# Two transformer blocks: the sums of squares shared between GpSimd and TensorE

## Chip, cores and metric

One core of one Trainium2 chip. The metric is the device time of one execution in microseconds.

## What is computed

Two transformer blocks of two layers each run one after the other on 512 tokens of width 1024 (the first also carries 256 context tokens in its first layer). Everything is fp32, and each large product is made of three matmuls on parts of the operands ("high" and "low"). Around every mixer and every feed-forward layer stand norms over the 1024 features of a token:

```
def rms_norm(x, g):
    xf = x.astype(jnp.float32)
    y = xf * lax.rsqrt(jnp.mean(xf * xf, axis=-1, keepdims=True) + EPS)
    return (y * g.astype(jnp.float32)).astype(x.dtype)

def modulate(x, g, shift, scale):
    return rms_norm(x, g) * (1 + scale) + shift
...
    h = h + gt_m * rms_norm(y, g_post_m)
    f = conv_ffn(modulate(h, g_pre_f, sh_f, sc_f), w_up[layer], ...)
    h = h + gt_f * rms_norm(f, g_post_f)
```

The second block's sliding-window attention adds a bias by distance, `rel_table[t5_bucket(rel)]`, which this kernel builds as a sum of 31 steps, each a `Sign` of the distance.

## The kernel before

**Layout.** Features lie on the partitions, in eight tiles of 128 features each (`K.h`, `K.y`: 128 x 8 x tokens), tokens along the free dimension: `TX` = 512, or `T0` = 768 with the context. A token's sum of squares therefore runs over eight tiles and over the partitions.

**Phases.** The program is a list of `Phase` objects. Each engine runs its own part of every phase in the order of that list, and counts of semaphores tie the parts together. Every engine is thus an in-order queue: what TensorE has in the next phase stands behind what it has in this one.

**Weights.** A chunk of 128 x 1024 weights is loaded by SyncE into one of six raw buffers (`load_chunk`), rounded by ScalarE to the high part (`split_hi`, L214) and subtracted by GpSimd to the low part (`split_lo`, L222). There are three buffers each for the high and the low parts (`HL`), so that chunk c+3 can be split once chunk c was used. TensorE waits for the low part (`chunk_ops`). L236 to L238 are the three matmuls of a large product. In the last layer before a norm some of these splits are put off behind the norm's root (`split_after`).

**Squares of the norms that this change touches.** `InnerNorm` (a norm of the layer's output, then the residual add, then the next norm) and `PreNorm` (the next norm alone) both inherit from `Squares`. There are nine. ScalarE squares tile k into a ring of two (768 tokens) or three (512) buffers in `K.t1` (`squared`, L674). GpSimd adds the eight squares one by one into `K.rstd` (`add`: L683 the first two, L686 each further one), and counts them in `y_used` or `sq_used`, on which ScalarE waits before it overwrites a buffer. Then TensorE makes one true fp32 product of `K.rstd` with a matrix of 1/1024 (`summed`, L700), which sums over the partitions and gives every partition the mean; and ScalarE takes the first root from PSUM (`first_root`, L709). VectorE improves it (L774, L780, L782 in `InnerNorm`, L846, L848, L850 in `PreNorm`) and makes the x tiles (L450, L459), each of which frees one step of the next layer's first product.

The squares are made while the layer before still ends. In a `Proj` phase (the output projections, and others) ScalarE's loop reads product i out of PSUM (L2645, where there is no gate), squares tile i and splits chunk i+3; with a gate VectorE reads the product (L867), and ScalarE splits first and squares tile i-1. GpSimd's loop adds square i-1 and then splits chunk i+3. After a feed-forward layer (`Ffn`) all eight squares follow VectorE's reads of the last eight products (L1309 or L867) inside `first_root` and `pool`.

The nine: after the even mixer's projection (768 tokens, root at 463 us), after its feed-forward layer (768, 1075), after the attention's projection (512, 1480), after that feed-forward layer (512, 1872), and five `PreNorm`: after a feed-forward layer at 2264, 2999 and 3374, after the projection with a gate at 2623 and 3729.

In `InnerNorm` TensorE goes on with `hold` (L165) and then the second norm's squares, one product each (L756). `warm` (L157) are matmuls whose result nobody reads: 22 of them at 512 tokens, in three groups, the second behind the first root and the third behind VectorE's first product; they stand ahead of the first product of the next layer.

**Signs.** `BiasTable(K, heads, tables, during, plan)`: ScalarE makes the 31 signs (L2082) in groups between its reads of the products of phase `during`; `plan[0]` before the first, `plan[i+1]` after product i. VectorE folds each into the sum (L2124). For the first table that phase is the projection of the values, with four products (L2650 reads them). For its third product TensorE needs a chunk that ScalarE splits after the second product, behind the signs of the first.

Of the kernel before, what the change touches and what calls it, by code (L numbers as in the profile page):

```python
# [29 lines left out]
TX = 512  # L30
TC = 256
T0 = TX + TC
# [30 lines left out]
def parts(T):  # L63

    return [(0, TX)] if T == TX else [(0, TX), (TX, TC)]
# [1 line left out]

EXTRA_SEMS = ["pe_gained", "mla_r", "qn_ready", "qc_ready", "gn_ready", "ang_ready", "cs_ready", "bias_ready", "bias_kept", "z_ready",
              "st_abs", "st_e", "st_nl", "a_ready", "lg_ready", "st_exp", "so_ready", "st_done", "mw_in", "rpb_in",
              "st_used", "table_in", "y_sq", "y_used", "y_total", "sq_total", "sq_sq", "mix_sq", "mix_total", "mix_r0", "mix_read", "mix_done", "begun_hi", "begun_lo", "rel_ready", "sign_ready", "sign_used"]  # L70
AREA = 4 * 4 * T0 + 3072


class Phase:
# [3 lines left out]
    def __init__(self, K):  # L78
        self.K, self.sem = K, K.sem
        self.base, self.c_next = dict(K.total), len(K.chunks)  # L80
        counts = self.counts()
        self.ring_before, K.ring_now = K.ring_now, None
        if "out_ready" in counts:
            K.ring_now = self.ring_T
        for name, n in counts.items():
            K.total[name] = K.total.get(name, 0) + n
        K.phases.append(self)

    def counts(self):
        return {}  # L90

    def at(self, name, n=0):

        return self.base.get(name, 0) + n
# [79 lines left out]
    def act(self, e): pass  # L174
    def dve(self, e): pass
    def pool(self, e): pass
# [30 lines left out]
def split_hi(K, act, c, n=0):  # L207
    if c >= len(K.chunks):
        return
    _, a, b, _ = K.chunks[c]  # L210
    act.wait_ge(K.sem[f"raw_in{c % RAW}"], 16 * (c // RAW + 1) + n * (16 * LC // RAW))
    if c >= HL:
        act.wait_ge(K.sem["out_ready"], K.chunks[c - HL][3] + n * LT)
    act.activation(K.whi[:, c % HL, 0:a * b], K.raw[:, c % RAW, 0:a * b], ACT.Copy).then_inc(K.sem["w_hi"], 1)  # L214


def split_lo(K, pool, c, n=0):
    if c >= len(K.chunks):
        return
    _, a, b, _ = K.chunks[c]  # L220
    pool.wait_ge(K.sem["w_hi"], c + 1 + n * LC)
    pool.tensor_tensor(K.wlo[:, c % HL, 0:a * b], K.raw[:, c % RAW, 0:a * b],  # L222
                       K.whi[:, c % HL, 0:a * b].bitcast(F32), ALU.subtract).then_inc(K.sem["w_lo"], 1)
# [188 lines left out]
class Modulated(Phase):  # L412
# [3 lines left out]
    def product(self, k):  # L416
        n = 2 if self.T == T0 else 3
        a = k % n * self.T
        return self.K.t2[:, :, :].rearrange("p a t -> p (a t)")[:, a:a + self.T]
# [45 lines left out]
class Norm(Modulated):  # L465
# [25 lines left out]
    def rstd_free(self, act):  # L491
        pass
# [156 lines left out]
class Squares:  # L649
# [2 lines left out]

    def begin(self, kind):
        self.kind, self.added, self.done, self.split_after = kind, 0, 0, []

    def square(self, k):
        n, T = (2, self.T) if self.T == T0 else (3, self.T)
# [2 lines left out]
    def squared(self, e, k):  # L662
        K, n = self.K, 2 if self.T == T0 else 3
        if k < 0:
            return
        if k == 0:
            e.preload_act_table_set("abs_reciprocal_sqrt_and_small")
            e.wait_ge(self.sem["act_lo"], self.act_lo)
        self.done = k + 1
        self.tile_done(e, k)  # L670
        if k >= n:
            used = self.kind + "_used"
            e.wait_ge(self.sem[used], self.at(used, k - n + 1))
        e.activation(self.square(k), self.tile(k), ACT.Square).then_inc(self.sem[self.kind + "_sq"], 1)  # L674

    def add(self, e, k):
        if k < 0:
            return
        self.added = k + 1
        acc, used = self.K.rstd[:, 0:self.T], self.kind + "_used"  # L680
        e.wait_ge(self.sem[self.kind + "_sq"], self.at(self.kind + "_sq", k + 1))
        if k == 1:
            e.tensor_tensor(acc, self.square(0), self.square(1), ALU.add).then_inc(self.sem[used], 2)  # L683
        elif k > 1:
            e.wait_ge(self.sem[used], self.at(used, k))
            e.tensor_tensor(acc, acc, self.square(k), ALU.add).then_inc(self.sem[used], 1)  # L686

    def pool(self, e):
        for k in range(self.added, 8):
            self.add(e, k)  # L690
        for c in self.split_after:
            split_lo(self.K, e, c)

    def summed(self, e):

        e.wait_ge(self.sem["ada_read"], self.ada_read)
        e.wait_ge(self.sem["bias_ready"], self.at("bias_ready"))
        e.wait_ge(self.sem[self.kind + "_used"], self.at(self.kind + "_used", 8))
        for a, w in parts(self.T):
            ins = e.matmul(self.total()[:, a:a + w], self.K.mean_d[:, :], self.K.rstd[:, a:a + w], start=True, stop=True)  # L700
        ins.then_inc(self.sem[self.kind + "_total"], 1)

    def first_root(self, e):

# [9 lines left out]
class InnerNorm(Squares, Norm):  # L714
# [2 lines left out]


    def __init__(self, K, T, post, pre, out):
        super().__init__(K, T, post, pre)  # L720
        self.act_lo, self.ada_read, self.tile_done, out.norm = self.at("act_lo"), K.ada_tasks, self.y_read, self
        self.begin("y")

    def counts(self):
        c = super().counts()
        c.update(self.ring_counts(self.T, 1))
        c.update(sq_ready=8, sq_used=7, y_sq=8, y_used=8, y_total=1)
        return c

    def total(self):  # L730
# [76 lines left out]
class PreNorm(Squares, Modulated):  # L807
# [2 lines left out]


    def __init__(self, K, pre):
        self.T, self.pre = TX, [pre]
        super().__init__(K)
        self.tile_done, self.ada_read, self.act_lo = K.h_done, K.ada_tasks, self.at("act_lo")
        self.begin("sq")
        K.phases[-2].norm = self

    def counts(self):
        return dict(sq_sq=8, sq_used=8, sq_total=1, r0_ready=1, xm_full=8, xm_hi=8, x_ready=8)  # L820

    def total(self):
        return self.K.pf[:, 6 * BANK:7 * BANK]
# [47 lines left out]
class Proj(Phase):  # L871
# [146 lines left out]
    def act(self, e):  # L1018
        T = self.T
        if self.table:  # L1020
            self.table.after(e, -1)
        for i, ((_, n, _, read), tok, own) in enumerate(self.products):
            if tok is None:
                if self.gate:
                    self.next_weights(e, i)
                    self.norm.squared(e, i - 1)
                    continue
                e.wait_ge(self.sem["out_ready"], self.at("out_ready", i + 1))
                read(e, self.slot(T, i)).then_inc(self.free(T, i), 1)
                if self.norm:  # L1030
                    self.norm.squared(e, i)
                self.next_weights(e, i)
                if self.table:
                    self.table.after(e, i)
            else:
                e.wait_ge(self.sem["out_ready"], self.at("out_ready", i + 1))
                for c in own if tok else ():
                    split_hi(self.K, e, c + HL)
                src = self.slot(T, i).rearrange("p (t c) -> p t c", t=self.half)[:, :, 0:n]
                read(e, src, tok).then_inc(self.free(T, i), 1)  # L1040
                if self.table:
                    self.table.after(e, i)
# [1387 lines left out]
class MlaNorm(Phase):  # L2430
# [40 lines left out]
    def pe(self, e):  # L2471
# [35 lines left out]
        while done < 9:  # L2507
            add(done)
            done += 1
# [138 lines left out]
def tokens_to(dst, col, func=ACT.Copy):  # L2648

    return lambda e, src, t: e.activation(dst[:, t:t + src.shape[1], col:col + src.shape[2]], src, func)  # L2650
# [11 lines left out]
def build(nc, io, out, stop=None):  # L2662
    K = Keep()
# [4 lines left out]
    with ExitStack() as ctx:  # L2668
# [54 lines left out]
        n = 4 * T0  # L2723
# [23 lines left out]
        def proj(T, w, jobs, wait=None, cls=Proj, **kw):  # L2747
            ph = cls(K, T, w, jobs, **kw)
            ph.warmed = wait is x_ready
            if wait:  # L2750
                ph.x_wait = lambda e, k: wait(ph, e, k)
            return ph
# [15 lines left out]
        first_table, first_pos = [at(4 * n, TX)], at(4 * n + 2560, TX).bitcast(I32)  # L2768
# [10 lines left out]
        proj(T0, w_in, jobs, tasks=mods[EARLY:5])  # L2779
        GmlpMix(K, gated)  # L2780
        v = proj(T0, w_in, [(2048 + g * 256, 256, True, tokens_to(K.vtok, g * 256)) for g in range(2)])
        table = BiasTable(K, [0], first_table, v, (0, 12, 12, 7))
        table.pos, table.posf = first_pos, at(4 * n + 2048, TX)
        split = Split(K, [K.sT[:, g, :] for g in range(4)], T0, "ya_done")

# [236 lines left out]
def finish(K, nc, out):  # L3022

    Store(K, out, out.shape[1])
    with nc.Block() as block:
        @block.sync
        def _(sp):
            for ph in K.phases:
                ph.sp(sp)

        @block.tensor
        def _(pe):
            for ph in K.phases:
                ph.pe(pe)

        @block.scalar
        def _(act):
            for ph in K.phases:
                ph.act(act)

        @block.vector
        def _(dve):
            for ph in K.phases:
                ph.dve(dve)

        @block.gpsimd
        def _(pool):
            for ph in K.phases:
                ph.pool(pool)
# [120 lines left out]
```

## Time and profile before

| what | us |
|---|---|
| runs before (3) | 4100.53, 4103.48, 4104.28; median 4103.48 |
| the profiled execution | 4102.06 |
| its span, first to last instruction | 4100.3 |
| TensorE busy, matmul | 3837.4 (94%) |
| VectorE, ScalarE, GpSimd busy | 1888.1, 1480.9, 1615.6 |

The span is what the trace covers; 1.8 us of the execution's time lie outside it. Matmuls are pipelined, so a busy TensorE isn't one at its peak. "L700" is line 700 of the kernel.

### The profile page before, as it was taken

Reading aid. Unit: us, or ns where it says so; the run is one execution under the profiler, and the core shown is the slowest. Engines: PE = TensorE matmul, PEld = TensorE weight load, DVE = VectorE, ACT = ScalarE, POOL = GpSimd, SP = SyncE. Lnnn points to the kernel's source line nnn. Section 1 sums busy time; section 2 is a strip of 40 time slices with the busy share of each in tenths; the row PEclk is TensorE's granted clock in tenths of the full one; section 3 lists DMA queues with packets and bytes.
Section 4 is the critical chain, followed back from the end, with each engine's and each line's share of the span. In section 5 each row is a group of like instructions: output and inputs, shape, how many; then the busy total and the mean of one; then the engine's idle time right before and its main releaser. Section 6 shows DMA issues by size and latency. Waiting matters only on the chain. (4 is left out here: it accounts for less than half of the span.)

```text
span 4100.3 us, 52392 instructions
## 1 busy us (share of the span) xinstructions
PE 3837.4 (94%) x19218; PEld 3035.1 (74%) x19218; DVE 1888.1 (46%) x3264; ACT 1480.9 (36%) x2293; POOL 1615.6 (39%) x801
## 2 busy tenths in 40 slices
PE   6987899999898899999999899999999999899999
PEld 5866688888666668887888753788878877547887
DVE  3775866543645556655554845222232232452222
ACT  3264522222325663333222554322232233533222
POOL 1320253444330046654455321455555553115554
PEclk9999999999999999999999998999999999989999
DMA  7610144442110027763665310233323332102332
GB/s 248 193 37 24 52 129 128 145 131 61 36 47 19 1 76 230 227 198 113 225 217 167 84 47 1 67 98 93 96 83 97 97 90 66 42 1 82 97 98 77
DMA packets 460503, 411.96 MB, mean 100 GB/s; under 512 B 28096, under 2 KB 405312, under 8 KB 460352
## 3 DMA queue, kind: packets, MB, share of 16 engines
q1 hardware_dynamic: 457903, 408.65, 32.3%
q8 instruction: 92, 1.51, 0.2%
q10 hardware_dynamic: 2448, 1.32, 0.1%
q14 instruction: 60, 0.48, 0.0%
HBM read 406.25 MB, written 7.60 MB: 101 GB/s over the span
## 5 line engine op out<-in xcount | busy, mean ns | idle before, releaser
L222 POOL TENSOR_TENSOR s_wlo<-s_raw,s_whi 128x1024 fp32r<-128x1024 f32 x490 | 1181.6, 2419 | 1927.4 <-ACT s_whi L214 1925.9
L236 PE MATMUL psum<-s_xhi,s_whi 128*128 128x512 f32 x3264 | 1227.5, 376 | 20.6 <-POOL s_wlo L222 11.0
L237 PE MATMUL psum<-s_xlo,s_whi 128*128 128x512 f32 x3264 | 1219.9, 374 | 0.0
L238 PE MATMUL psum<-s_xhi,s_wlo 128*128 128x512 f32 x3264 | 1216.5, 373 | 0.0
L214 ACT ACTIVATE s_whi<-s_raw 128x1024 fp32r<-128x1024 f32 x490 | 510.1, 1056 | 1533.8 <-PE psum L238 1530.5
L236 PEld LDWEIGHTS psum<-s_xhi,s_whi 128*128 128x128 f32 x3264 | 615.6, 189 | 139.8 <-POOL s_wlo L222 13.4
L237 PEld LDWEIGHTS psum<-s_xlo,s_whi 128*128 128x128 f32 x3264 | 615.5, 189 | 111.4 <-issue 3.6
L238 PEld LDWEIGHTS psum<-s_xhi,s_wlo 128*128 128x128 f32 x3264 | 614.6, 188 | 111.9
L236 PE MATMUL psum<-s_ahi,s_whi 128*128 128x512 f32 x1232 | 469.0, 381 | 11.6 <-DVE s_y L1309 7.2
L238 PE MATMUL psum<-s_ahi,s_wlo 128*128 128x512 f32 x1232 | 464.8, 377 | 0.0
L237 PE MATMUL psum<-s_alo,s_whi 128*128 128x512 f32 x1232 | 462.4, 375 | 0.0
L1297 DVE TENSOR_TENSOR s_t<-psum,s_t 128x512 f32<-128x512 f32 x88 | 60.9, 692 | 842.0 <-ACT s_t L1255 842.0
L867 DVE SCALAR_TENSOR_TENSOR s_h<-psum,s_coef,s_h 128x512 f32<-128x512 f32 x368 | 268.8, 749 | 198.5 <-PE psum L238 184.6
L236 PEld LDWEIGHTS psum<-s_ahi,s_whi 128*128 128x128 f32 x1232 | 232.8, 189 | 58.1 <-DVE s_y L1309 7.8
L238 PEld LDWEIGHTS psum<-s_ahi,s_wlo 128*128 128x128 f32 x1232 | 232.7, 189 | 46.3
L237 PEld LDWEIGHTS psum<-s_alo,s_whi 128*128 128x128 f32 x1232 | 232.7, 189 | 44.4
L384 DVE CUSTOM_DVE_ANT_0 s_ada_raw<-s_ada_raw,psum 128x1024 f32<-128x1024 f32 x176 | 214.0, 1216 | 54.3 <-DMA s_ada_raw<-w_ada 43.8
L1285 DVE SCALAR_TENSOR_TENSOR s_t<-psum,s_cols,s_t 128x511 f32<-128x511 f32 (+1 forms) x132 | 82.9, 655 | 324.8 <-ACT s_t L1252 324.8
L1343 POOL TENSOR_TENSOR s_alo<-s_t,s_ahi 128x512 fp32r<-128x512 f32 (+1 forms) x132 | 183.5, 1390 | 37.4 <-ACT s_ahi L1262 37.4
L1623 PE MATMUL psum<-s_ident,s_t 128*128 128x128 f32 x772 | 131.7, 294 | 69.8 <-DVE s_t L1748 35.1
L1681 ACT ACTIVATE s_area<-psum 128x512 f32<-128x512 f32 (+1 forms) x212 | 123.1, 581 | 148.1 <-PE psum L1623 147.9
L1623 PEld LDWEIGHTS psum<-s_ident,s_t 128*128 128x128 f32 x772 | 84.8, 146 | 120.6 <-issue 65.1
(306 smaller groups left out, 4274.9 us busy)
## 6 DMA issues: line engine op xcount, KB each, us to landing
s_ada_raw<-w_ada SPq DMA_DIRECT2D x224, 512.0 KB, 3.9
s_raw<-w_gu SPq DMA_DIRECT2D x176, 512.0 KB, 3.8
s_raw<-w_up SPq DMA_DIRECT2D x88, 512.0 KB, 4.7
s_raw<-w_dn SPq DMA_DIRECT2D x88, 512.0 KB, 3.5
s_raw<-w_down SPq DMA_DIRECT2D x44, 512.0 KB, 4.6
s_raw<-w_in SPq DMA_DIRECT2D x30, 512.0 KB, 3.9
s_raw<-w_in_ab SPq DMA_DIRECT2D x20, 512.0 KB, 6.6
s_area<-w_first SPq DMA_DIRECT2D x16, 512.0 KB, 11.9
```

Of the source, the lines that this page charges most:

```text
L214: act.activation(K.whi[:, c % HL, 0:a * b], K.raw[:, c % RAW, 0:a * b], ACT.Copy).then_inc(K.sem["w_hi"], 1)
L222: pool.tensor_tensor(K.wlo[:, c % HL, 0:a * b], K.raw[:, c % RAW, 0:a * b], K.whi[:, c % HL, 0:a * b].bitcast(F32), ALU.subtract).then_inc ...
L236: pe.matmul(out, lh, rh, start=first, stop=False)
L237: pe.matmul(out, lh, rl, start=False, stop=False)
L238: return pe.matmul(out, ll, rh, start=False, stop=last)
L384: ins = dve.tensor_tensor_reduce(out=chunk if v == last else K.ada_acc[:, 0, :], in0=chunk, in1=self.rows.row(v), scale=1.0, scalar=0.0, o ...
L867: return e.scalar_tensor_tensor(out=K.h[:, m, 0:TX], in0=product, scalar=K.coef[:, m:m + 1], in1=K.h[:, m, 0:TX], op0=ALU.mult, op1=ALU.add)
L1285: ins = e.scalar_tensor_tensor(out=dst[:, a + 1:a + w], in0=src[:, a:a + w - 1], scalar=K.cols[:, bass.ds(c, 1)], in1=dst[:, a + 1:a + w], ...
L1297: e.tensor_tensor(K.t1[:, i, 0:T], self.slot(T, t - 1), K.t2[:, i, 0:T], ALU.mult).then_inc(self.sem["prod"], 1)
L1343: e.tensor_tensor(K.alo[:, j % 2, i, 0:T], K.t1[:, i, 0:T], K.ahi[:, j % 2, i, 0:T].bitcast(F32), ALU.subtract).then_inc(self.sem["act_lo" ...
L1623: ins = e.transpose(self.t(4)[:, i * P:(i + 1) * P], self.p(s, j)[:, b * P:(b + 1) * P], K.ident[:, :])
L1681: e.activation(self.pt(s, 4 * c, m), self.t(m), ACT.Copy).then_inc(self.sem["t_copied"], 1)
```

## The change

The first tiles' squares are still added by GpSimd: seven of them where the norm follows a projection (`Proj`), five after the feed-forward layer of 768 tokens, six after those of 512. TensorE multiplies the remaining squares with the matrix of 1/1024 itself and accumulates in PSUM. `order` says in which order TensorE takes them; `None` is GpSimd's sum. A new semaphore (`y_seen`, `sq_seen`) counts the squares that TensorE has read. In `Proj` without a gate ScalarE splits the next chunk before it squares the tile. The first table's signs are dealt out 0, 9, 14, 8 instead of 0, 12, 12, 7.

```diff
@@ class Squares
-    def begin(self, kind):
-        self.kind, self.added, self.done, self.split_after = kind, 0, 0, []
+    def begin(self, kind, adds):
+        self.kind, self.added, self.done, self.split_after, self.adds = kind, 0, 0, [], adds
+        self.order = {7: (None, 7), 6: (6, 7, None), 5: (5, 6, None, 7)}[adds]
+
+    def kind_counts(self):
+        return {self.kind + "_sq": 8, self.kind + "_used": self.adds, self.kind + "_total": 1,
+                self.kind + "_seen": sum(k is not None for k in self.order[:-1])}
@@ squared
         if k >= n:
-            used = self.kind + "_used"
-            e.wait_ge(self.sem[used], self.at(used, k - n + 1))
+            name, past = (self.kind + "_used", 0) if k - n < self.adds else (self.kind + "_seen", self.adds)
+            e.wait_ge(self.sem[name], self.at(name, k - n + 1 - past))
@@ add
-        if k < 0:
+        if k < 0 or k >= self.adds:
             return
@@ pool
-        for k in range(self.added, 8):
+        for k in range(self.added, self.adds):
@@ summed
-        e.wait_ge(self.sem[self.kind + "_used"], self.at(self.kind + "_used", 8))
-        for a, w in parts(self.T):
-            ins = e.matmul(self.total()[:, a:a + w], self.K.mean_d[:, :], self.K.rstd[:, a:a + w], start=True, stop=True)
-        ins.then_inc(self.sem[self.kind + "_total"], 1)
+        def product(x, first, last):
+            for a, w in parts(self.T):
+                ins = e.matmul(self.total()[:, a:a + w], self.K.mean_d[:, :], x[:, a:a + w], start=first, stop=last)
+            return ins
+
+        for k in self.order:
+            if k is None:
+                e.wait_ge(self.sem[self.kind + "_used"], self.at(self.kind + "_used", self.adds))
+            else:
+                e.wait_ge(self.sem[self.kind + "_sq"], self.at(self.kind + "_sq", k + 1))
+            ins = product(self.K.rstd if k is None else self.square(k), k == self.order[0], k == self.order[-1])
+            if k == self.order[-1]:
+                ins.then_inc(self.sem[self.kind + "_total"], 1)
+            elif k is not None:
+                ins.then_inc(self.sem[self.kind + "_seen"], 1)
@@ InnerNorm.__init__
+        self.begin("y", 7 if isinstance(out, Proj) else 5 if T == T0 else 6)
@@ PreNorm.__init__
+        self.begin("sq", 7 if isinstance(out, Proj) else 6)
@@ Proj.act
                 read(e, self.slot(T, i)).then_inc(self.free(T, i), 1)
+                self.next_weights(e, i)
                 if self.norm:
                     self.norm.squared(e, i)
-                self.next_weights(e, i)
@@ build
-        table = BiasTable(K, [0], first_table, v, (0, 12, 12, 7))
+        table = BiasTable(K, [0], first_table, v, (0, 9, 14, 8))
```

## Rows read from the trace of the kernel before

**Rows 1.** Busy time in the span by engine; the core's span and mean granted clock.
```profile
PE 3837.4 (94%) x19218; PEld 3035.1 (74%) x19218; DVE 1888.1 (46%) x3264; ACT 1480.9 (36%) x2293; POOL 1615.6 (39%) x801
...
core 0: 4100.3 us, clock 0.972
```
**Rows 2.** The product line L700: durations min/median/max, and its waits (us, times).
```profile
L700 PE MATMUL psum<-s_rstd,s_mean_d x22: 631/1061/1193, 460.0 to 3727.6; 128*128 128x512 f32 x18, 128*128 128x256 f32 x4
...
  POOL s_rstd L686: 48.4, 9
```
**Rows 3.** Timeline, 2253 to 2272: start, us, what, count, [idle before <- releaser].
```profile
2253.69 8.38 POOL L686 TENSOR_TENSOR s_rstd<-s_rstd,s_t 128x512 f32<-128x512 f32 x6
...
2257.94 0.63 ACT L674 ACTIVATE s_t<-s_h 128x512 f32<-128x512 f32 x1 [0.78 <-POOL s_rstd L686]
...
2262.21 2.04 PE L700 MATMUL psum<-s_rstd,s_mean_d 128*128 128x512 f32 x2 [5.41 <-POOL s_rstd L686]
2263.27 8.00 PE L157 MATMUL psum<-s_whi 128*128 128x512 f32 x22
2271.10 0.39 PE L236 MATMUL psum<-s_xhi,s_whi 128*128 128x512 f32 x1
...
2264.29 0.69 ACT L709 ACTIVATE s_rstd<-psum,s_eps 128x512 f32<-128x512 f32 x1 [5.72 <-PE psum L700]
...
2268.81 0.75 DVE L459 SCALAR_TENSOR_TENSOR s_xlo<-psum,s_mod,s_xhi 128x512 fp32r<-128x512 f32 x1
```
**Rows 4.** Stretches: busy PE, PEld, DVE, ACT, POOL (count), granted clock, DMA share, GB/s.
```profile
2260.00:2262.00 2.00, 0.00 (x0) 0.00 (x0) 0.00 (x0) 0.00 (x0) 1.86 (x2) 0.88 0.80 218
...
2268.00:2270.00 2.00, 2.00 (x10) 1.60 (x9) 1.90 (x4) 1.35 (x2) 2.00 (x2) 0.91 0.23 28
```
**Rows 5.** Timeline of the mixer behind that norm.
```profile
2284.75 1.16 ACT L2048 ACTIVATE s_area<-s_area 128x512 f32<-128x512 f32 x2 [5.92 <-DVE s_area L2042]
...
2289.82 0.50 PE L236 MATMUL psum<-s_xhi,s_whi 128*128 128x512 f32 x1 [2.24 <-POOL s_wlo L222]
```
**Rows 6.** Timeline, norm behind the feed-forward layer of 768 tokens.
```profile
1060.52 11.71 POOL L686 TENSOR_TENSOR s_rstd<-s_rstd,s_t 128x768 f32<-128x768 f32 x6 [1.01 <-ACT s_t L674]
...
1072.37 2.90 PE L700 MATMUL psum<-s_rstd,s_mean_d 128*128 128x512 f32 x4 [5.33 <-POOL s_rstd L686]
...
1082.47 1.53 PE L756 MATMUL psum<-s_t,s_mean_d 128*128 128x512 f32 x4 [0.57 <-ACT s_t L502]
```
**Rows 7.** Timeline, second norm at 1881: eight products in a row.
```profile
1880.99 7.59 PE L756 MATMUL psum<-s_t,s_mean_d 128*128 128x512 f32 x16
```
**Rows 8.** Timeline, norm behind the even mixer's projection.
```profile
453.79 2.35 POOL L222 TENSOR_TENSOR s_wlo<-s_raw,s_whi 128x1024 fp32r<-128x1024 f32 x1 [1.25 <-ACT s_whi L214]
456.10 3.74 POOL L686 TENSOR_TENSOR s_rstd<-s_rstd,s_t 128x768 f32<-128x768 f32 x2
...
459.98 2.90 PE L700 MATMUL psum<-s_rstd,s_mean_d 128*128 128x512 f32 x4 [10.10 <-POOL s_rstd L686]
```
**Rows 9.** Timeline, norm behind the attention's projection.
```profile
1475.12 2.68 POOL L686 TENSOR_TENSOR s_rstd<-s_rstd,s_t 128x512 f32<-128x512 f32 x2
...
1477.95 2.05 PE L700 MATMUL psum<-s_rstd,s_mean_d 128*128 128x512 f32 x2 [5.57 <-POOL s_rstd L686]
```
**Rows 10.** Timeline, norm behind a projection with a gate.
```profile
2619.40 1.26 POOL L686 TENSOR_TENSOR s_rstd<-s_rstd,s_t 128x512 f32<-128x512 f32 x1 [0.35 <-ACT s_t L674]
...
2620.81 2.04 PE L700 MATMUL psum<-s_rstd,s_mean_d 128*128 128x512 f32 x2 [2.94 <-POOL s_rstd L686]
```
**Rows 11.** Timeline of the first table's signs, and one stretch with its clock.
```profile
227.50 1.99 ACT L214 ACTIVATE s_whi<-s_raw 128x1024 fp32r<-128x1024 f32 x2
...
231.68 7.98 ACT L2082 ACTIVATE s_t<-s_t,s_cols 128x512 f32<-128x512 f32 x10 [0.28 <-DVE psum L2124]
...
231.11 0.55 PE L236 MATMUL psum<-s_whi,s_xhi 128*128 128x256 f32 x1 [5.21 <-POOL s_wlo L222]
...
230.00:232.00 2.00, 0.89 (x4) 0.93 (x5) 1.07 (x2) 1.72 (x4) 2.00 (x2) 0.65 0.00 0
```

More of the change, by code:

```diff
@@ L69 @@
               "st_abs", "st_e", "st_nl", "a_ready", "lg_ready", "st_exp", "so_ready", "st_done", "mw_in", "rpb_in",
-              "st_used", "table_in", "y_sq", "y_used", "y_total", "sq_total", "sq_sq", "mix_sq", "mix_total", "mix_r0", "mix_read", "mix_done", "begun_hi", "begun_lo", "rel_ready", "sign_ready", "sign_used"]
+              "st_used", "table_in", "y_sq", "y_used", "y_total", "sq_total", "y_seen", "sq_seen", "sq_sq", "mix_sq", "mix_total", "mix_r0", "mix_read", "mix_done", "begun_hi", "begun_lo", "rel_ready", "sign_ready", "sign_used"]
 AREA = 4 * 4 * T0 + 3072
@@ L719, in __init__ @@
     def __init__(self, K, T, post, pre, out):
+        self.begin("y", 7 if isinstance(out, Proj) else 5 if T == T0 else 6)
         super().__init__(K, T, post, pre)
         self.act_lo, self.ada_read, self.tile_done, out.norm = self.at("act_lo"), K.ada_tasks, self.y_read, self
-        self.begin("y")
     def counts(self):
@@ L726, in counts @@
         c.update(self.ring_counts(self.T, 1))
-        c.update(sq_ready=8, sq_used=7, y_sq=8, y_used=8, y_total=1)
+        c.update(sq_ready=8, sq_used=7, **self.kind_counts())
         return c
@@ L812, in __init__ @@
     def __init__(self, K, pre):
-        self.T, self.pre = TX, [pre]
+        self.T, self.pre, out = TX, [pre], K.phases[-1]
+        self.begin("sq", 7 if isinstance(out, Proj) else 6)
         super().__init__(K)
         self.tile_done, self.ada_read, self.act_lo = K.h_done, K.ada_tasks, self.at("act_lo")
-        self.begin("sq")
-        K.phases[-2].norm = self
+        out.norm = self
     def counts(self):
-        return dict(sq_sq=8, sq_used=8, sq_total=1, r0_ready=1, xm_full=8, xm_hi=8, x_ready=8)
+        return dict(r0_ready=1, xm_full=8, xm_hi=8, x_ready=8, **self.kind_counts())
     def total(self):
```

## The prediction

> **What bounds the kernel now.** I first read the page's list of busy time: TensorE is busy for 3837 of 4100 us [rows 1]. So time can be won only where TensorE waits, or where it runs at its lower clock. I then looked up the lines that the diff touches. The product line (L700) has 22 matmul records for its nine norms, and before these TensorE waited 48.4 us in all for GpSimd [rows 2]. That is the most that removing the adds alone could give, about 1.2%. An fp32 product of 512 columns makes two records: 7 norms of 512 columns make 14 and the two of 768 columns, which are 512 and 256, make 8.
>
> Last I read the timeline around each norm; rows 3 show one of the four at the end of a 512-token feed-forward layer (1855, 2247, 2982 and 3357 us; at 1855 the same pattern, with an `InnerNorm`). The last square ends at 2258.57. GpSimd's six adds take 1.40 each (8.38 / 6) and end only at 2262.07. TensorE, idle for 5.41, then needs 2.04 for one product, and ScalarE's root starts at 2264.29. After it VectorE's chain gives the first x tile at 2269.56 (2268.81 + 0.75). TensorE starts the next product only at 2271.10, because 22 warming matmuls took 8.00 from 2263.27. The granted clock shows why both are slow: [rows 4] have it at 0.88 over 2260 to 2262, thus it fell to 1.2 GHz at about 2261.5, and it is 0.91 over 2268 to 2270, thus back at 2.4 GHz from about 2268.4.
>
> **The change, place by place.** The price of a product comes first. At the lower clock one of 512 columns takes 2.04 alone, one of 768 columns 2.90 [rows 3, 6]; 256 columns more cost 0.86, so one that follows another costs 1.72 or 2.58, without the start. At 2.4 GHz eight in a row take 7.59, 0.95 each [rows 7], and one of 768 columns 1.53 alone [rows 6], about 1.4 in a row. So an extra product is cheaper than the add of 1.40 at one clock and dearer at the other: the clock decides the size.
>
> The Trainium skill says the same against the change ("FP8 and Floating Point Precision", TensorE Precision Notes): true fp32 goes through the array in four passes. By it the extra product of 512 columns is an estimated 4 x 512 / 1.2 GHz = 1.7, dearer than the add it replaces. The trace agrees: 1.72.
>
> *Feed-forward, 512 tokens, four places (adds 6).* GpSimd now ends after five instructions of its chain: 2253.69 + 4 x 1.40 = 2259.3. TensorE, which has just ended its last product at 2256.8 (2262.21 - 5.41), takes square 6 at 2257.3, square 7 at 2258.7 and the sum at 2259.7, because square 7's product ends then; it is done by 2260.8 instead of 2264.25. The idle stretch is gone, so I take 2.4 GHz. The root comes **3.5** earlier [rows 3]. If the clock were low throughout, three products would end at 2257.3 + 2.04 + 2 x 1.72 = 2262.8, a gain of 1.5. What hangs on it differs:
> - 2982 (next a feed-forward layer): with the clock up, warming ends before the first x tile, so the start moves from 1.5 behind it to just after it. 3.5 + 1.4 = 4.9, I take **4.8** (bounds 1.5 and 5.0).
> - 2247 and 3357 (next the mixer): TensorE soon waits anyway. At 2289.82 it waits 2.24 for GpSimd's low part, which stands behind ScalarE's sine, which stands behind VectorE's chain [rows 5]. Only the shift of VectorE's chain counts: 3.5 each, **7.0** (3.0 and 7.2).
> - 1855 (`InnerNorm`): the second norm's eight products end at 1888.58 [rows 7], about 0.6 later than VectorE's tiles ask for, because the hold before them ran partly at 1.2 GHz. 3.5 + 0.6 = **4.1** (1.5 and 4.2).
>
> *Feed-forward, 768 tokens (adds 5, at 1075).* Adds take 1.95 (11.71 / 6) and the fourth and last is done at 1066.4, before TensorE's last product ends at 1067.04 (1072.37 - 5.33) [rows 6]. Then TensorE does four products of 768 columns in a row: 1067.1 + 4 x 1.4 + 0.2 = 1072.9 against 1075.27. The new wait of square 7 is for the product of square 5 (about 1068.6); it ends in time, since its own product comes last. Gain **2.3**; at the low clock four end at 1067.1 + 2.90 + 3 x 2.58 = 1077.7, a loss of 2.4.
>
> *Projection, 768 tokens (adds 7, at 460).* Split before square brings GpSimd's L222 from 453.79 to 452.95; it ends at 455.3 and one add of 1.87 at 457.2. TensorE starts at 457.3 instead of 459.98, but it has been idle since 449.88 and has a second product to do: at 1.2 GHz 2.90 + 2.58 end at 462.8 against 462.88 [rows 8]. Gain **0.1**; were the clock up, 2.7. Moved past the square the split can't hold ScalarE, since its weights were loaded six chunks ahead.
>
> *Projection of attention, 512 tokens (at 1478).* GpSimd loses an add (1.34) and its split starts about 0.6 earlier, a square of 0.63 as in [rows 3]: TensorE starts at 1476.0 instead of 1477.95 [rows 9]. The extra product takes 0.95 or 1.7, the first 1.1 or 2.04. That gives 2.0 or 0.3. After 4.2 idle I can't tell the clock: **1.2**.
>
> *Projections with a gate (2620 and 3726).* The order on ScalarE is unchanged. The last add starts at 2619.40 after 0.35 idle, so the seventh tile is in at 2619.05; TensorE starts at 2619.2 and ends two products at 2621.3, or 2622.9 at 1.2 GHz, against 2622.85 [rows 10]. That is 1.55 or -0.1; if the clock stays up the warming gives 1.4 as above. Between -0.1 and 3.0 I take 2.2, as the idle stretch shrinks from 2.94 to 1.3: **4.4** for both.
>
> *Signs (at 218 to 252).* A sign costs 0.80 [rows 11]. With 9 instead of 12, ScalarE is free 2.4 earlier, but its split also waits for TensorE's second product (225.9, since 231.11 - 5.21). So split and all behind it move from 227.50 to 226.1: 1.4. TensorE then starts at 229.7. Before, the clock was 0.65 over 230 to 232, so it fell at about 230.6 and TensorE did its first 2.9 us at half rate; if it doesn't fall, 1.4 more. The 14 signs then end at about 240, the 8 at 247, each beside a product of TensorE. **2.4** (1.4 and 2.8).
>
> Sum: 4.8 + 7.0 + 4.1 + 2.3 + 0.1 + 1.2 + 4.4 + 2.4 = **26.3**. The profiled execution took 4102.06 (span 4100.3), so 4075.8 on its scale; the median of the runs is 1.4 higher. I say **4076.5**. All low bounds of the clock together give 5.2, all high ones 32.4.
>
> **The rivals.**
> - *The products run at 1.2 GHz everywhere.* For it: today every L700 does. Against it: that follows an idle stretch of 2.9 to 10 us, and in five places there is none any more. Gain 5.2: 4097, no measurable change. Chance 0.05.
> - *Half is given back behind the norms*: the stages after them wait for something that doesn't move, as at 2289.82. Only the places before a feed-forward layer or a chain I followed would keep theirs (4.8 + 4.1 + 4.4 = 13.3): 4089. For it: the mixer's many waits; against: these are waits of engine for engine, which move along. Chance 0.12.
> - *The adds are not what ends the squares* (the change doesn't do what it says): the sum would still wait. Against it stand 48.4 us of waits for GpSimd alone [rows 2]. 4102. Chance 0.02.
> - *Slower: every later stretch meets the clock at another moment.* The whole kernel spends about 230 us at 1.2 GHz (mean clock 0.972 [rows 1]). Waits inside the attention stages that now just escape could fall. One fall costs about 3 (6 us at half rate, as from 2262.21 to 2268.4 [rows 4]). Twelve new ones would eat 26.3 and 8 more: 4112. It decides from nine on. Nothing favours new falls over vanished ones. Chance 0.03.
>
> **Numbers.** My forecast has 0.78, with its own range 4069 to 4084. The range of 8 in 10 takes in the second rival: 4069 to 4090. A measurement of this kernel can tell about 0.2% (8.2 us) from no change. Faster by more: 0.78 + 0.12 = 0.90; within: 0.07; slower: 0.03.
>
> **What the profile after would show.** Right: in the four 512-token feed-forward ends six product records follow the last L238 with gaps under 1 us at clock 1.00, the root 4.0 after that L238's end instead of 7.5; warming x22 in about 5.3 instead of 8; at 231 TensorE's wait near 3.7 and its clock not falling; at 460 nothing gained. Wrong if the clock is 0.50 over the new products, or if L236's waits behind the norms grow by what the root gained.

## The result, and the profile after

The changed kernel took 4073.26 us in the median of four runs (4067.20 to 4078.39), the kernel before 4103.46 in four (4100.53 to 4104.28). The ratio is 0.9926, with a 95% interval of 0.9911 to 0.9942: 24 to 37 us less, clear of the noise and under 1%. I had said 4076.5. The profiled execution took 4078.39 (span 4076.5) against 4102.06: 23.7 less, where my sum was 26.3. It is at the slow end of the four.

The page after, answering to [rows 1], and then the product line, answering to [rows 2] (durations min/median/max, then its waits: us, times):

```profile
PE 3844.3 (94%) x19256; PEld 3036.2 (74%) x19256; DVE 1885.3 (46%) x3264; ACT 1480.1 (36%) x2293; POOL 1593.1 (39%) x786
...
core 0: 4076.5 us, clock 0.976
```

```profile
L705 PE MATMUL psum<-s_t,s_mean_d x38: 378/592/1061, 459.0 to 3705.2; 128*128 128x512 f32 x30, 128*128 128x256 f32 x8
...
L705 PE MATMUL psum<-s_rstd,s_mean_d x22: 379/592/1193, 456.3 to 3704.4; 128*128 128x512 f32 x18, 128*128 128x256 f32 x4
...
  POOL s_rstd L691: 14.8, 8
  ACT s_t L679: 7.6, 12
```

TensorE has 15 more products (38 records) and GpSimd 15 fewer adds. The waits for GpSimd fell from 48.4 to 14.8, those for squares are new at 7.6; and the median product takes 0.59 where it took 1.06: most of them now run at 2.4 GHz. The granted clock over the span rose from 0.972 to 0.976.

The place of [rows 3 and 4] after the change, timeline and stretches:

```profile
2247.46 1.10 PE L705 MATMUL psum<-s_t,s_mean_d 128*128 128x512 f32 x2 [0.49 <-ACT s_t L679]
...
2248.78 1.13 PE L705 MATMUL psum<-s_t,s_mean_d 128*128 128x512 f32 x2 [0.22 <-ACT s_t L679]
...
2249.74 1.02 PE L705 MATMUL psum<-s_rstd,s_mean_d 128*128 128x512 f32 x2
...
2250.80 0.69 ACT L725 ACTIVATE s_rstd<-psum,s_eps 128x512 f32<-128x512 f32 x1 [2.07 <-PE psum L705]
```

```profile
2250.20 5.83 PE L157 MATMUL psum<-s_whi 128*128 128x512 f32 x22
2256.22 0.47 PE L236 MATMUL psum<-s_xhi,s_whi 128*128 128x512 f32 x1 [0.18 <-DVE s_xlo L459]
```

```profile
2248.00:2250.00 2.00, 1.78 (x5) 0.67 (x4) 0.03 (x1) 0.63 (x1) 1.27 (x2) 1.00 0.23 81
```

This is the picture that I had forecast: six records, gaps of 0.49 and 0.22, clock 1.00 (over 2246 to 2248 too), and the root 3.8 behind the end of the last large product (2247.46 - 0.49 = 2246.97; forecast 4.0, before 7.5). The sum of GpSimd is no longer late: nothing stands before its product. And TensorE now waits for VectorE's first x tile (0.18), where before the x tile waited 1.5 for the warming matmuls.

**A measure for each place.** The time from the end of the last large product ahead of a norm to the start of the first one behind it holds all that the norm costs, and nothing of what came before. At [rows 3] it was 2271.10 - (2262.21 - 5.41) = 14.30 (14.29 before rounding); after the change it is 2256.22 - 2246.97 = 9.25. I call it the norm's stretch and take it at all nine places in the same way:

| root before | forecast | stretch before | after | gain |
|---|---|---|---|---|
| 463 | 0.1 | 44.77 | 44.14 | 0.6 |
| 1075 | 2.3 | 41.59 | 38.52 | 3.1 |
| 1480 | 1.2 | 30.74 | 29.81 | 0.9 |
| 1872 | 4.1 | 30.74 | 26.53 | 4.2 |
| 2264 | 3.5 | 14.29 | 9.25 | 5.0 |
| 2623 | 2.2 | 11.73 | 8.73 | 3.0 |
| 2999 | 4.8 | 14.09 | 9.26 | 4.8 |
| 3374 | 3.5 | 14.05 | 9.55 | 4.5 |
| 3729 | 2.2 | 11.73 | 8.73 | 3.0 |
| signs | 2.4 | 49.58 | 48.26 | 1.3 |

For the signs it is the time between the last large products of the phases around them (200.33 to 249.91, then 200.09 to 248.35). The gains come to 30.5, 4 more than I forecast. The span gained only 23.8, so 6.7 were given back between these places. The feed-forward layers gave back about 1.0 (of 512 tokens: two before 2264 are equal to 0.01, two later ones longer by 0.1, the last by 0.4; that of 768 tokens by 0.4), the stretch between the signs and 450 gave back 1.4, the mixer behind 2264 1.0 and the last mixer 4.8; the attention stage gained 1.2. The last mixer shows it best. One stretch for each kernel, from the first to the last large product of that mixer (busy times as in [rows 4], then the granted clock, DMA share, GB/s); before:

```profile
3380.70:3723.70 343.00, 313.06 (x1493) 204.70 (x1491) 138.60 (x341) 145.76 (x329) 89.03 (x51) 0.94 0.15 43
```

After:

```profile
3354.70:3702.60 347.90, 317.02 (x1492) 207.75 (x1492) 140.84 (x343) 146.49 (x329) 90.17 (x52) 0.92 0.15 43
```

The same work took 4.9 longer at a granted clock of 0.92 instead of 0.94. The first new fall is at the wait that answers to [rows 5]:

```profile
2276.32 0.80 PE L236 MATMUL psum<-s_xhi,s_whi 128*128 128x512 f32 x1 [3.50 <-POOL s_wlo L222]
```

```profile
2276.00:2278.00 2.00, 1.68 (x4) 1.39 (x5) 1.97 (x2) 0.71 (x1) 2.00 (x2) 0.50 0.27 48
```

The kernel before, behind the wait of [rows 5]:

```profile
2290.00:2292.00 2.00, 2.00 (x9) 1.61 (x10) 1.97 (x2) 0.20 (x1) 2.00 (x1) 1.00 0.42 89
```

TensorE starts the mixer 5.0 earlier against the last layer, VectorE's chain only 3.65 (the root), so the wait for the low part grew from 2.24 to 3.50, and behind it the clock is 0.50, where it had stayed at 1.00. The product behind this wait starts 25.5 behind the root in both kernels (2289.82 - 2264.29, 2276.32 - 2250.80): up to there the mixer keeps the root's shift and nothing else.

### The profile page after: what moved, and what is told of

The parts are those of the page before. It is cut to its first block, busy times and chain, and to the rows that moved or that the text cites. A ratio compares the mean times of both kernels' runs of the same rounds, so it can differ in the third digit from the quotient of the medians.

```text
span 4076.5 us, 52438 instructions
## 1 busy us (share of the span) xinstructions
PE 3844.3 (94%) x19256; PEld 3036.2 (74%) x19256; DVE 1885.3 (46%) x3264; ACT 1480.1 (36%) x2293; POOL 1593.1 (39%) x786
## 3 DMA queue, kind: packets, MB, share of 16 engines
q1 hardware_dynamic: 457903, 408.65, 32.4%
## 4 chain that ended last, share of the span: by engine, by line
PE 55%; issue 17%; POOL 13%; DVE 8%; ACT 5%; DMA 1%; POOLq 0%; ACTq 0%; DVEq 0%; SPq 0%
PE psum L236 15%; PE psum L237 14%; PE psum L238 14%; POOL s_wlo L222 10%; POOL s_alo L1359 2%; PE psum L1639 2%; PE psum L1650 1%; ACT s_t L1687 1%; PE psum L1627 1%; PE psum L1618 1%; DVE s_stat L1754 1%; DVE s_t L1764 1%; POOL s_rstd L691 1%; DVE s_h L814 1%; PE psum L2536 1%
```

## The experiments

Each kernel was timed in 5 rounds against the kernel before (5 to 11 executions). Ratios are to the kernel before on the same chip, and x 4102 gives the microseconds behind them. They are not quotients of the two medians; the two ways of reckoning differ by up to 3.6 us.

**The change again.** No edit; it shows how far two executions of one program differ.

> The changed kernel, unchanged, once more. Its four first runs spread over 11 us (4067 to 4078), those of the kernel before over 4 us. Theory: the nine norms keep their gain in every run and the spread comes from stretches at the lower granted clock elsewhere; so the median lies again at 4066 to 4080 (ratio 0.991 to 0.995), and the profile shows the same steps at the norms (3.6 for each feed-forward end of 512 tokens) while the total time at 1.2 GHz differs by up to 30 us between executions. Rival: the gain itself is a matter of the clock's luck; then the steps at the norms differ too, by over 1 us.

Measured: 4075.39 (4071.32 to 4080.21), ratio 0.9935 [0.9921, 0.9949]. The stretches are those of the table to 0.1, except at 1480 (32.5 instead of 29.8), and the last mixer took 345.0, not 347.9. The mixer behind 2264 took 345.3, not 347.8. So the stretches of the norms repeat but for that at 1480, and what moves an execution by several microseconds lies there and in the mixers.

**The sums alone**, twice: before's order of split and square, and before's signs.

```diff
-                self.next_weights(e, i)
                 if self.norm:
                     self.norm.squared(e, i)
+                self.next_weights(e, i)
...
-        table = BiasTable(K, [0], first_table, v, (0, 9, 14, 8))
+        table = BiasTable(K, [0], first_table, v, (0, 12, 12, 7))
```

> Only the sums are shared with TensorE (7, 5 and 6 adds by GpSimd); squares stand ahead of the split and the signs are 0, 12, 12, 7 as before. Theory: nearly all of the gain is here, 24 to 29 us (ratio 0.993 to 0.994): 3.5 at each of four feed-forward ends and what the clock adds behind them, 2.3 at the one of 768 tokens, about 1 to 2 at the others. Rival (split and signs carry the gain): under 10 us.

> The kernel with the sums alone once more. Theory A and rival B: again 4081 to 4084, 19 below before. Rival C (scatter of where the clock falls in the attention stage and in the last mixer, which moves a whole execution by up to 10): nearer 4077, and the stretches over the nine norms are the same to 0.2 as in its first run: 45.4, 38.5, 30.9, 26.5, 9.3, 8.7, 9.3, 9.6, 8.7.

Measured: 4083.09, ratio 0.9950 [0.9936, 0.9963] (20.5 us), and 4080.77, 0.9940 [0.9927, 0.9954] (24.6). The stretches from 2264 on are those of the whole change to 0.02 in both; that at 463 is 45.4 and 45.3, at 1480 30.9 and 32.7. So the sums are about four fifths of the gain. The first two stretches of the second run, and the last five, repeat those of the first to 0.1; the two between differ by 1.5 and 1.8, so the last expectation holds in seven of nine.

**The split alone**, in the kernel before (the first hunk above, reversed).

> The kernel before with the split ahead of the square in the two projections without a gate, all eight adds by GpSimd. Theory: GpSimd's last add ends 0.84 earlier at the 768-token projection and about 0.6 earlier at the attention's, so 1.4 us in all, not measurable in the time (ratio 0.9995), but visible at the two roots in the trace. Rival (the square behind the split comes too late for GpSimd): a loss of up to 0.8 at each of them.

Measured: 4098.12, ratio 0.9990 [0.9981, 0.9999]: 4.1, between 0.4 and 7.8. In its trace the root comes 1.6 sooner behind the last large product at 463 and 0.1 sooner at 1480, and TensorE's waits for low parts inside the attention's projection fall from 1.7 to 0.8. But the two stretches gained nothing (44.8 and 32.2, before 44.8 and 30.7), and that profiled execution took 4102.94. So the waits show the split, the stretches don't.

**The signs alone**, in the kernel before.

> The kernel before with the signs dealt out 0, 9, 14, 8. Theory: 1.4 us from TensorE's third product on, 2.8 if the clock doesn't fall there; ratio 0.9995, near the limit of what can be told. The trace of the changed kernel already shows the wait shortened from 5.21 to about 3.7 and the clock falling all the same, so I expect 1.4. Rival: the 14 signs delay what comes behind and the step is gone by the attention: 0.

Measured: 4102.33, ratio 0.9997 [0.9988, 1.0006]. In the trace the time between the two phases around the signs is 48.27 instead of 49.58. That is 1.3, as in every kernel with the new dealing, and less than this timing can tell. And it is gone before the next norm. Behind the signs TensorE waits 2.87 for ScalarE in every kernel, and 16 small matmuls follow; in the kernel before and in the changed one:

```profile
252.78 2.85 PE L1611 MATMUL psum<-s_area 64*128 64x256 f32 x16 [2.87 <-ACT s_area L2650]
```

```profile
251.22 4.36 PE L1627 MATMUL psum<-s_area 64*128 64x256 f32 x16 [2.87 <-ACT s_area L2666]
```

Over 252 to 254 the granted clock is 1.00 before and 0.50 after. All seven profiles with the new dealing have this fall, and none of the seven with the old one. With the signs alone, the time from the large product ahead of them to the last one ahead of the norm at 463 is 249.6, as before. So the rival's outcome holds (the step is gone, 0), though by the clock and not by late signs.

**The sums with the split, and the sums with the signs**, to part the two further.

> The new sums and the split ahead of the square, with the signs dealt out as before (0, 12, 12, 7). The sums alone gave 19.4, everything together 27 to 30, while the split alone gave 4.4 and the signs alone 0.2. Theory A (each place has its own gain and they add): against the sums alone the idle stretch between the last layer product before the norm at 460 and the first behind it shrinks from 45.4 to about 44.1 (1.3), and the signs' 1.4 are missing against the whole change: 4102 - 26 = 4076. Rival B (the signs are what the sums alone lacked): no better than the sums alone, 4082. Rival C (the sums alone were only at the low end of their scatter): 4079, and the sums alone, run again, the same.

> The new sums and the new dealing of the signs, with the split behind the square as before. Theory A: against the sums alone 1.4 at the signs and nothing at the norms: 4080 to 4081; the stretch over the norm at 460 stays at 45.4. Rival B (the signs carry the missing part): 4075. Rival C: 4077, with the sums alone at 4078 when run again.

Measured: 4075.79, ratio 0.9931 [0.9917, 0.9944] (28.3), and 4079.69, 0.9941 [0.9928, 0.9955] (24.2). So to the sums (20.5 and 24.6) the split adds 4 to 8, and the signs lie 2 beyond the mean of the two, with an interval of 5 to either side. The three medians of this chip (4075.79, 4079.69, 4080.77) lie as theory A had them, but their intervals overlap, so the timing favours theory A over rival B without deciding it. The traces speak against rival B, since the signs' 1.3 is given back before the norm at 463.

The split seems worth more than I had seen. It doesn't only bring the last chunk earlier but all of them: TensorE's waits for low parts from 1425 to 1479 are 1.7 in the kernel before, 1.6 and 1.8 with the sums alone, and 0.8 with sums and split, as with the split alone. That is 0.9 in the projection; the stretches at 463 and 1480 are 0.9 and 1.1 shorter than in the better of the two runs of the sums alone. Together 2.9. That it reaches the total isn't shown: the attention stage as a whole took 363.4 and 359.0 in the two profiles of the sums alone.

**Only the sums behind feed-forward layers**: eight adds at the projections as before.

```diff
-        self.begin("sq", 7 if isinstance(out, Proj) else 6)
+        self.begin("sq", 8 if isinstance(out, Proj) else 6)
```

> The sums are shared only behind the five feed-forward layers (5 adds at 768 tokens, 6 at 512); behind the four projections GpSimd adds all eight as before; split and signs as before. Theory: 2.3 + 4.1 + 3.5 + 4.8 + 3.5 = 18 us (ratio 0.9955), the larger part of the whole. Rival (each norm of the nine gives the same): five ninths of 30, 16 us, with the roots behind the projections of 512 tokens giving over 3 each.

Measured: 4080.67, ratio 0.9952 [0.9939, 0.9966] (19.7). The stretches at 1075, 1872, 2264, 2999 and 3374 gain 3.1, 4.2, 5.0, 4.8 and 4.5, as in the whole change; that at 3729 gains nothing, that at 2623 gains 2.3, since the clock stayed up there this time. The five places behind feed-forward layers carry nearly all that the sums bring.

**The kernel before, with TensorE kept busy while it waits for the adds.** All eight adds stay; small matmuls whose result nobody reads stand ahead of that wait. It parts the clock from the adds.

```diff
+        for _ in range(self.fill):          # 16; 8 behind projections with a gate
+            e.matmul(self.total()[:, 0:P], self.K.mean_d[:, :], self.K.mean_d[:, :], start=True, stop=True)
         e.wait_ge(self.sem[self.kind + "_used"], self.at(self.kind + "_used", 8))
```

> The kernel before, where TensorE makes 16 (behind a projection with a gate 8) products of 128 columns that nobody uses while it waits for GpSimd's sum; they are overwritten. This takes away the fall of the clock and leaves the wait. Theory: the one product then takes 1.10 instead of 2.04 and the 22 warming matmuls 5.3 instead of 8: 0.9 at each root of 512 tokens, and 1.4 more where a feed-forward layer follows a PreNorm (three times); together 8 to 11 us (ratio 0.9975). So about a third of the whole change would be the clock. Rival 1 (the waits for the adds are all of it): 0 to 2 us. Rival 2 (the fillers end after the adds and delay the product): slower.

Measured: 4091.50 (4088.62 to 4102.41), ratio 0.9984 [0.9975, 0.9993] (6.6; the profiled execution, 4088.62, is the fastest of eleven). The place of [rows 3] in it:

```profile
2252.86 3.73 PE L699 MATMUL psum<-s_mean_d 128*128 128x128 f32 x32
2258.35 1.12 PE L702 MATMUL psum<-s_rstd,s_mean_d 128*128 128x512 f32 x2 [1.75 <-POOL s_rstd L686]
2258.91 5.84 PE L157 MATMUL psum<-s_whi 128*128 128x512 f32 x22
```

The product takes 1.12 instead of 2.04, though it waits for the same adds, and warming 5.8 instead of 8.0. The stretches of the four feed-forward ends of 512 tokens gain 1.6, 2.4, 2.2 and 2.1, those behind gated projections 2.3 each. So of the 4.8 at 2999, 2.2 is the clock and 2.6 what sharing the adds brings beyond it; of the 3.0 at 2623, 2.3 and 0.7. Here too the last mixer took 346.4, not 343.0: of the 17.7 that the nine stretches gained, the timing shows 3 to 10.

**Six adds everywhere.** At the projections `order` is `(None, 6, 7)`, at 768 tokens behind the feed-forward layer `(6, None, 7)`.

```diff
-        self.begin("sq", 7 if isinstance(out, Proj) else 6)
+        self.begin("sq", 6, (None, 6, 7) if isinstance(out, Proj) else (6, 7, None))
```

> The changed kernel with six adds everywhere: order sum, 6, 7 behind projections; 6, sum, 7 behind the 768-token feed-forward layer; 6, 7, sum behind the others. Theory: behind projections TensorE no longer waits for a split on GpSimd that stands between the adds of squares 5 and 6: 2.7 at the attention's root, 0.45 at each of the two with a gate, 0 at the 768-token one (where the start is earlier but the clock is low and one more product of 2.58 is made); 1.3 at the 768-token feed-forward end (one product of 1.4 less). Together 4.9 us below the changed kernel. Rival: an extra product costs as much as the wait that it saves: 0.

Measured: 4066.07 (4064.75 to 4074.42), ratio 0.9919 [0.9906, 0.9933]. The norm behind the attention's projection, to be read beside [rows 9]:

```profile
1463.80 1.10 PE L705 MATMUL psum<-s_rstd,s_mean_d 128*128 128x512 f32 x2 [0.52 <-POOL s_rstd L691]
```

The add that still stood behind the last split is gone, TensorE's wait of 5.57 (4.04 in the changed kernel) is 0.52, and the root comes 3.4 behind the last large product, not 6.7. Behind the gated projections it comes after 2.7 instead of 3.3, at 1075 after 4.4 instead of 5.2. At 463 nothing is gained (11.2 against 10.8): there TensorE does one more product, the first at 1.2 GHz.

**The same, with `hold` ahead of the wait at 463**: 21 matmuls once the tile before is read.

```diff
+        if self.fill:
+            e.wait_ge(self.fill[0], self.fill[1])
+            self.hold(e, 21, 5)
         e.wait_ge(self.sem["bias_ready"], self.at("bias_ready"))
```

> As the kernel with six adds everywhere, and behind the 768-token projection TensorE makes 21 matmuls of 512 columns on weights (results unused) from the end of its last product until the sum is there. Theory: the clock stays at 2.4 GHz over the three products (1.5 + 1.4 + 1.4 from about 452.4), the root comes near 457 instead of 460.5: 3.5 us below the kernel with six adds. Rival: the sum isn't ready before 456, so that only the clock's part of about 2 us is won, or the held matmuls end later than the sum.

Measured: 4066.07 (4064.05 to 4069.02), ratio 0.9911 [0.9897, 0.9925]. Its first product, where [rows 8] have 2.90:

```profile
455.44 1.45 PE L708 MATMUL psum<-s_rstd,s_mean_d 128*128 128x512 f32 x4
```

```profile
454.00:456.00 2.00, 2.00 (x10) 1.49 (x9) 1.90 (x6) 1.32 (x2) 1.52 (x1) 1.00 0.14 52
```

The clock stays at 1.00, the stretch is 40.4 instead of 44.6, and the median doesn't move: against six adds alone the timing can't tell the 4 from nothing. Both versions have medians 7 to 9 below the changed kernel's, though their intervals still touch its.

**A later start of the mixers.** In the kernel with six adds everywhere, 28 instead of 22 warming matmuls ahead of the two mixers, to try the reason that I had for the falls.

```diff
+            ph.more = 6
...
-            for _ in range(n):
+            for _ in range(n + (more if value else 0)):
```

> The kernel with six adds everywhere, and six more warming matmuls (22 become 28, about 1.3 us) ahead of the first product of the two mixers that follow a PreNorm. The whole change starts that product 5.4 behind the root instead of 6.8, while ScalarE and GpSimd behind VectorE's chain only move with the root: so TensorE's wait for GpSimd's low part 20 us later grew from 2.24 and 2.49 to 3.5, and behind it the clock is 0.51 for 6.8 us, where before it stayed at 1.00. Theory A (that fall is new and takes back what the earlier start won, and more): the later start costs nothing, the wait goes back to 2.2 to 2.5, the clock stays at 1.00 behind it, and each mixer ends 1.5 to 3 earlier: 4066 - 3 to - 6 = 4060 to 4063; the stretches from the first layer product behind the roots at 2264 and 3374 to the last one of the mixer are 2 to 3 shorter than in the kernel with 22. Rival B (the clock falls there whatever the wait): the 1.3 is won back in the wait, no more, 4066. Rival C (a start that is later is simply later): 4066 + 2.6 = 4069.

Measured: 4071.90 (4061.95 to 4074.42), ratio 0.9921 [0.9908, 0.9935], where 22 gave 0.9919. Behind the first of the two mixers' waits (2.58, the product at 2271.49):

```profile
2272.00:2274.00 2.00, 2.00 (x6) 1.53 (x5) 1.99 (x1) 0.00 (x0) 2.00 (x1) 0.50 0.66 161
```

The wait shrank from 3.53 to 2.58, and the clock fell all the same. The mixers took 348.1 and 348.3, where they took 345.5 and 345.2 with 22. Theory A falls: the longer wait isn't what brings the clock down there, or not alone. The kernel with the sums only behind feed-forward layers shows it from the other side, at the last mixer:

```profile
3378.54 0.50 PE L236 MATMUL psum<-s_xhi,s_whi 128*128 128x512 f32 x1 [3.53 <-POOL s_wlo L222]
```

```profile
3380.00:3382.00 2.00, 2.00 (x10) 1.65 (x9) 0.00 (x0) 0.00 (x0) 2.00 (x2) 1.00 0.88 241
```

A wait of 3.53 left the clock up. Rival B holds as far as that product: it starts 25.5 behind the root with 28 warming matmuls as with 22, so the later start is won back in the wait. Whether it costs something further on (rival C, 4069) the timing can't tell.

## Why the prediction was right, and where it wasn't

**The mechanism.** Right at seven of the nine norms, the five feed-forward ends and the two gated projections: TensorE's own products filled the idle stretch or shortened it, they ran at 2.4 GHz, and so one of 512 columns cost 1.02 to 1.13 instead of 2.04. At 463 the first product still ran at 1.2 GHz, and at 1480 one profile of the changed kernel had its first product at 2.4 GHz and the other both at 1.2. In the stretches at 463, 1075 and 1480 the clock still falls; from the other six the fall is gone. In all nine stretches together TensorE was at 1.2 GHz for about 71 us before and 17 after; outside them it was for 157 before and 178 after, which goes with what was given back. The warming matmuls took 5.83, where I had 5.3. The first rival (products at 1.2 GHz everywhere) and the third (adds that don't end the squares) are refuted by the rows above: clock 1.00 and a GpSimd wait of nothing. The kernel with the filled wait shows the clock's part by itself: about half of the gain at a feed-forward end, three quarters behind a gated projection.

The Trainium skill ("FP8 and Floating Point Precision", TensorE Precision Notes) has true fp32 as four passes. At 2.4 GHz and one column per clock that is an estimated 4 x 512 / 2.4 = 0.85, less than the add of 1.40 that it replaces; the trace's 1.02 with its start, and 0.95 in a row [rows 7], are somewhat longer. So its rule spoke against the change only at the lower clock.

**The terms.**
- 2999 and 1872: 4.8 and 4.1 forecast, 4.8 and 4.2 measured. In two of the later kernels 1872 gained only 2.6.
- 2264 and 3374: 3.5 each forecast, since only VectorE's chain should count. The stretches gained 5.0 and 4.5; behind them the wait grew by 1.3 (2.24 to 3.50) and 1.0 (2.49 to 3.53), as that argument said. What I did not have is the clock's fall behind those waits.
- 2623 and 3729: 2.2 each, 3.0 measured: the clock stayed up in full.
- 1075: 2.3, 3.1 measured: four products of 768 columns cost 5.3 (1066.47 to 1071.79), not 5.8.
- 463: 0.1, 0.6 measured, by two things that I did not have. The root came 2.2 sooner (10.8 behind the last large product, 13.0 before): the first product ran at 1.2 GHz (2.90) as forecast, the second at 2.4 (1.53, where I had 2.58), and GpSimd's sum was ready 0.9 sooner. Then 1.6 of it was given back between the root and the next large product, where the clock fell once more (0.60 over 486 to 488; before, 1.00 throughout 484 to 492).
- 1480: 1.2, 0.9 measured, but in the second profile of the same kernel the stretch was 1.8 longer than before. Behind the wait the two products took 1.10 and 1.70 in the one and 2.04 and 1.91 in the other, so I was right that the clock can't be told there, and the term stays open. My idle time of 4.2 did not follow from my own start (1476.0 - 1472.4 = 3.6); 4.04 was measured. The split was mis-sized: I priced only its last step, and it also takes 0.9 off the waits inside the projection. Timed, it brings about 4 alone and 4 to 8 beside the sums, of which the traces show 2.9 at most.
- Signs: 2.4, 1.3 measured at the place and nothing left of it at the next norm. TensorE's wait fell from 5.21 to 3.75 as forecast (3.7), but the clock fell all the same (0.60 over 230 to 232, [rows 11]), and it fell once more at 251, which took 1.5.

The high bounds add up to 32.2, not 32.4.

**What was given back.** The second rival, that half is lost behind the norms, was right in part and by another mechanism. In the two mixers that follow a feed-forward end the profiled execution lost 1.0 and 4.8, and behind the signs it lost 1.4 by the fall at 251. These losses go with the clock. The last mixer took 343.0 at 0.94, 345.0 at 0.93 and 347.9 to 348.4 at 0.92, in kernels whose instructions there are the same.

It took 343.0 in the kernel before and in the two that change nothing at the norms, and 344.0 to 348.4 in all eleven profiles of kernels that do, the one with the filled wait among them. For the mixer behind 2264 there is no such order: 346.6 to 346.8 in those three, and 344.9 to 351.3 in the eleven. The longest, 351.3, is in the second run of the sums alone, where the wait was 3.51 and the clock stayed up behind it. So a later stage can lose 1 to 5 us to the clock, or win some, when something ahead of it ends sooner; that a norm which ends sooner always costs is not shown. My fourth rival had this mechanism (later stretches meet the clock at another moment), at 3 for each fall; the falls at six norms that went away outweighed it. Why the clock falls at some waits and not at others of the same length stays open.

Two errors thus offset each other, and the nearness of 4076.5 to the profiled 4078.39 is in part luck: the terms of the sum were 4 too small, and nothing stood in it for the 6.7 that other stages gave back.

## What to carry to other kernels

When TensorE idles ahead of a small product on the critical path, ask first what its clock is there: filling the idle time with useful products can be worth as much as the work that they take over. Judge each edit over a stretch that begins and ends on TensorE's own work at that place, since a total also holds what the clock does elsewhere; and then time the kernel, and look at the next wait behind the place, since a local gain may be given back there: the signs' 1.3 was lost 3 us later. An order in which every engine's last piece ends at the same time (six adds here, five to seven in the change) is found by looking at who still waits.

## What the hardware showed that I had not expected

The untouched last mixer takes between 343.0 and 348.4 us, and its length goes with its granted clock (0.94 to 0.92); two executions of the changed kernel had 347.9 and 345.0. Unchanged programs spread by 10 us over their runs (before 4097.61 to 4107.74 in one series of 21), so edits worth 1 to 4 us could be read only in the traces.

The length of a wait doesn't tell by itself whether the clock falls. At the same instruction 2.24 us left it at 1.00, 2.58 did not, and 3.51 did; at the last mixer 3.53 left it at 1.00 in one kernel and brought it to 0.50 in another. Behind the signs the same wait of 2.87 brought it down in all seven profiles with the new dealing and in none with the old.
